# Causal mask of the first attention: added in the accumulator by VectorE instead of a TensorE product of the unit matrix with the mask

## The reference

```python
s = jnp.einsum("bhqd,bhkd->bhqk", qi, kh).astype(jnp.float32) * scale
s = s + ci[..., :, None] - c[:, :, None, :]
q_pos = i * Q_BLOCK + jnp.arange(Q_BLOCK)
s = jnp.where(k_pos[None, :] <= q_pos[:, None], s, -jnp.inf)
p = jax.nn.softmax(s, axis=-1).astype(vh.dtype)
return jnp.einsum("bhqk,bhkd->bhqd", p, vh)
```

## Time and profile before

| | |
|---|---|
| median of 3 runs | 2807.35 us |
| lowest, highest | 2804.43, 2808.54 us |
| span of the profiled execution | 2800.1 us |
| TensorE busy | 2668.2 us, 95% |
| VectorE busy | 1814.9 us, 65% |
| ScalarE busy | 1261.1 us, 45% |
| GpSimd busy | 400.7 us, 14% |
| mean granted clock of TensorE | 0.984 of full |

### The profile page before, as it was taken

The page is one execution under the profiler, slowest core; times in us unless marked ns, Lnnn a source line. Parts: engine busy times, 40 slices in busy tenths (PEclk is TensorE's granted clock), DMA queues, the critical chain, the costliest instruction groups (busy, mean ns, idle before and its releaser), DMA issues. The chain is left out here.

```text
span 2800.1 us, 35787 instructions
## 1 busy us (share of the span) xinstructions
PE 2668.2 (95%) x13585; PEld 2229.8 (80%) x13585; DVE 1814.9 (65%) x2331; ACT 1261.1 (45%) x1900; POOL 400.7 (14%) x578
## 2 busy tenths in 40 slices
PE   8999999999999999999999999989999499999995
PEld 7788888888897777778888898868878488888884
DVE  4277776632347888884343542378854798888887
ACT  4244443421244333333232422168842377777774
POOL 2011110000021222221010220012231300000102
PEclk9999999999999999999999999999999799999998
DMA  5100010111323435547441632000233699999996
GB/s 182 34 24 12 12 35 16 53 54 52 113 84 104 137 115 159 163 140 277 155 143 53 184 87 64 20 20 20 72 122 125 247 376 395 393 396 394 396 396 237
DMA packets 245593, 424.40 MB, mean 152 GB/s; under 512 B 15164, under 2 KB 161328, under 8 KB 245424
## 3 DMA queue, kind: packets, MB, share of 16 engines
q1 hardware_dynamic: 222304, 349.06, 35.3%
q0 software_dynamic: 23008, 73.03, 8.2%
q10 hardware_dynamic: 112, 0.03, 0.0%
HBM read 367.48 MB, written 45.14 MB: 147 GB/s over the span
## 5 line engine op out<-in xcount | busy, mean ns | idle before, releaser
L497 PE MATMUL ps<-r,r 128*128 128x512 f32 (+2 forms) x10448 | 2302.9, 378 | 21.5 <-ACT f L786 4.4
L497 PEld LDWEIGHTS ps<-r,r 128*128 128x128 f32 x10448 | 1870.0, 189 | 375.9 <-issue 14.7
L474 ACT ACTIVATE r<-f 128x2048 fp32r<-128x2048 f32 (+2 forms) x319 | 486.2, 1531 | 422.5 <-PE ps L497 405.0
L3541 DVE TENSOR_TENSOR r<-f,r 128x2048 fp32r<-128x2048 f32 x188 | 429.3, 2292 | 63.7 <-ACT r L474 62.6
L482 DVE TENSOR_TENSOR r<-f,r 128x1024 fp32r<-128x1024 f32 (+1 forms) x131 | 144.6, 1117 | 372.3 <-ACT r L474 371.9
L497 PE MATMUL ps<-f,f 128*128 128x64 f32 (+3 forms) x1410 | 218.4, 304 | 0.4 <-DVE f L3489 0.3
L497 PEld LDWEIGHTS ps<-f,f 128*128 128x128 f32 (+1 forms) x1410 | 179.5, 192 | 23.2 <-issue 19.6
L831 DVE SCALAR_TENSOR_TENSOR f<-f,misc,f 128x1023 f32<-128x1023 f32 (+29 forms) x120 | 146.4, 1262 | 0.0
L1764 DVE SCALAR_TENSOR_TENSOR f<-f,misc,f 128x256 f32<-128x256 f32 x224 | 128.6, 594 | 8.4 <-DMA f<-in_w_ada_dram 6.1
L1909 ACT ACTIVATE r<-f 128x512 fp32r<-128x512 f32 x140 | 87.6, 629 | 76.4 <-PE ps L497 63.2
L1115 ACT ACTIVATE f<-ps,misc 128x128 f32<-128x128 f32 (+7 forms) x64 | 47.5, 742 | 146.1 <-DVE misc L1104 146.1
(11 more groups left out here) (335 smaller groups left out, 2112.2 us busy)
## 6 DMA issues: line engine op xcount, KB each, us to landing
f<-in_w_gate_dram SPq DMA_DIRECT2D x64, 1024.0 KB, 8.6
f<-in_w_up_dram SPq DMA_DIRECT2D x64, 1024.0 KB, 10.3
f<-in_w_down_dram SPq DMA_DIRECT2D x64, 1024.0 KB, 8.4
f<-in_w_in_dram SPq DMA_DIRECT2D x56, 512.0 KB, 4.5
f<-in_w_ada_dram SPq DMA_DIRECT2D x48, 512.0 KB, 3.9
f<-hid_scratch SPq DMA_DIRECT2D x44, 512.0 KB, 5.2
f<-in_w_ffn_in_dram SPq DMA_DIRECT2D x80, 256.0 KB, 4.5
x_scratch<-f POOLq DMA_DIRECT2D x24, 512.0 KB, 5.1
```

Source lines behind the costliest of these rows:

```text
L474: self.act.activation(hi, raw, ACT.Copy).then_inc(self.sem(st.name + "_hi"), 1)
L497: return self.pe.matmul(o, left, right, start=start, stop=stop, skip_group_check=True)
L3541: self.dve.tensor_tensor(es.lo[i % 4], es.raw[i % 8], es.hi[i % 4].bitcast(F32), ALU.subtract).then_inc(self.sem("e_lo"), 1)
```

## The change

The product with the mask is gone from `pe_scores`; each score product now closes its own group, and the last one raises `at_qk`. In `dve_largest` VectorE, after its waits, adds the mask (fp32, as GpSimd made it) to the last 128 columns in the accumulator, raises a new semaphore `at_mask`, waits for it itself, and then takes the maximum. ScalarE's rounding of the mask at the start is gone, with its count of `round`.

```diff
-    (("round", 2), ("n1_sq", 8), ("pj_v", 32), ("a2_val", 32), ("hi_hi", 32)),
+    (("round", 1), ("n1_sq", 8), ("pj_v", 32), ("a2_val", 32), ("hi_hi", 32)),
...
-        self.ident_r, self.mask_r = [nc.alloc_sbuf_tensor_at(f"round{j}", [P, P], F32R, offset=base + 201 * 1024 + j * P * 4)
-                                     for j in (0, 3)]
+        self.ident_r = nc.alloc_sbuf_tensor_at("round0", [P, P], F32R, offset=base + 201 * 1024)
...
         act.activation(self.ident_r[:, 0:P], self.eye, ACT.Copy).then_inc(sem("round"), 1)
-        act.activation(self.mask_r[:, 0:P], self.mask, ACT.Copy).then_inc(sem("round"), 1)
...
-        pe.wait_ge(*sem("round", 2))
+        pe.wait_ge(*sem("round", 1))
...
             w = min(512, kw - c0)
-            diag = c0 + w == kw
             o = self.ps[:, b0 + c0 // 512, 0:w]
-            m = self.mm(o, self.QT[0:66, h, i * P:(i + 1) * P], self.KT[0:66, h, c0:c0 + w], True, not diag)
-            if diag:
-                m = self.mm(o[:, w - P:w], self.ident_r[:, 0:P], self.mask_r[:, 0:P], False, True)
+            m = self.mm(o, self.QT[0:66, h, i * P:(i + 1) * P], self.KT[0:66, h, c0:c0 + w], True, True)
         m.then_inc(sem("at_qk"), 1)
...
-        dve.tensor_reduce(self.nmax[u % 2], self.scores_of(u)[1], AX.X, ALU.max, negate=True).then_inc(
-            sem("at_max"), 1)
+        scores = self.scores_of(u)[1]
+        diagonal = scores[:, self.UNITS[u][0] * P:]
+        dve.tensor_tensor(diagonal, diagonal, self.mask, ALU.add).then_inc(sem("at_mask"), 1)
+        dve.wait_ge(*sem("at_mask", 16 * g + u + 1))
+        dve.tensor_reduce(self.nmax[u % 2], scores, AX.X, ALU.max, negate=True).then_inc(sem("at_max"), 1)
```

## The result

The changed kernel takes 2817.76 us (median of 6 runs, 2814.78 to 2820.77), the kernel before 2807.31 us on the same chip. The ratio is 1.0038 with a 95% interval of 1.0026 to 1.0049: slower by 10.5 us, 7 to 14 by the interval. The forecast was 2819.2, 11.8 us slower.

A forecast was written before the change was run, and what follows sets the result against it. A loop through VectorE's reduce, ScalarE's queue and TensorE bounds the attention. Per head pair 3.84 - 0.48 - 0.27 = 3.09 us, four make 12.4, less 0.6 gives 11.8; 2807.35 + 11.8 = 2819.2 us, range 2811.5 to 2828.

The forecast's parts named there:

- Rival (a): First attention: TensorE sets the pace, adds fall into VectorE's idle time, 3.8 us saved, 2803.5; chances 0.03 faster, 0.03 within.
- the 0.32 of the forecast: VectorE before each reduce: add 0.285 us plus 0.035 for the semaphore wait makes the maximum 0.32 us later per step.
- Rival (c): VectorE's add costs 0.425 us because it must write the accumulator as well as read it; 6.7 us more, 2826; chance 0.13.
- 12 of 16 per head pair: Attention adds on the path: u=1, 2, 4, 7 swallowed, the other 12 count, u=0 included; 12 x 0.32 = 3.84 us.
- the idle time before u=6: VectorE's gap before the reduce of u=6 swallows 0.21 us per head pair, with 0.06 in smaller gaps.
- the tail's 0.6: Last five units of head pair 3: some 0.1 us per step hides behind TensorE's previous matmul, 0.6 us less.
- as said for u=1: Add of u=1 in each head pair swallowed: VectorE next waits 0.51 us at L1182 for TensorE's values.
- 8 x 0.06 x 4: Removed mask products give back 0.06 us at eight units per head pair where the path runs through the scores.
- The rest at nothing: Mask rounding at the start gains nothing, at most 0.5 us; behind the attention everything shifts along, else up to 11.8 could vanish.
- (b): Attention: the loop binds everywhere, no add swallowed, no product back; 64 x 0.32 = 20.5 us, 2827.8; chance 0.12.
- (d): Attention: more is swallowed, only the 32 wide steps count, 6.9 or 4.5 us, 2812 to 2814; chance 0.15.
- (e): TensorE's clock: longer waits in the attention cause one drop to 1.2 GHz, costing about 4 us, 2823; chance 0.03.

The follow-up runs named there:

- the run with both: Kernel before, keeping its mask product, with the add and its wait also put ahead of the reduce; stretch 341.3 us, median 2821.6, ratio 1.0045.
- the first profile: Kernel before, unchanged, the profile on which the forecast rests; stretch from first to last reduce of the attention 329.4 us, span 2800.1.
- the second profile: Kernel before, unchanged, profiled once more for the spread between executions; stretch from first to last reduce of the attention 328.7 us.

## Why the prediction was right, step by step

**The mechanism.** TensorE is held behind the reduce by way of ScalarE's queue; the add lengthens that chain. Shown: the waits grew at the two places named, the loss is there with the product in place, and it vanishes (0.4 us the other way, within the spread) when one of the two copies is taken from behind the exponential. Rival (a), TensorE sets the pace, is out; so is its record of 465 ns. The product was worth 0.050 to 0.061 us. The 81 ns of the Trainium skill (TensorE: Matmul & The Clock Gate, section on the back-to-back issue gap), which would make 5.2 us of the 3.2 to 3.9, are not borne out here.

**The add.** It took 0.299 us and the reduce began 0.034 behind it; a step of 0.334 against the 0.32 of the forecast. Rival (c), 0.425 for a write into the accumulator, is out: writing the accumulator cost 0.015 us more than writing SBUF in L1032's group. The estimate of 0.42 per step from the Trainium skill (Perfetto Trace Analysis, section Optimizing Scalar/DVE Operations) is out with it.

**Which adds count.** This is the step of the sum that was off. The forecast had 12 of 16 per head pair, 3.84 less 0.27 of idle time. I followed the finish of the reduces unit by unit through the run with both, in head pair 2: u=0 and u=1 add 0.33 and 0.34, by u=2 and u=3 0.31 of that is gone again, and u=4, 7 and 9 to 15 add 0.31 to 0.34 each. That makes 3.31 us. The forecast's own sum, without the products and with 0.334, is 12 x 0.334 - 0.27 = 3.74. Of the 0.43 too many, 0.334 is u=0, which I had let count through the wide transposes. The other 0.09 is a misreading of the idle time before u=6: an instruction of VectorE that waits for nothing begins 0.09 before the one ahead ends, so the 0.21 of the earlier trace rows had room for 0.30. The failure at u=0 can be read from the trace. Before the change (head pair 2, the same step) TensorE waited twice in a row:

```profile
310.45 0.42 PEld L1133 LDWEIGHTS ps<-round,f 128*128 128x128 f32 x4 [0.44 <-ACT f L1142]
...
311.19 0.14 PEld L1063 LDWEIGHTS ps<-round,f 128*66 128x66 f32 x2 [0.32 <-ACT f L1013]
```

and after it

```profile
315.82 0.42 PEld L1131 LDWEIGHTS ps<-round,f 128*128 128x128 f32 x4 [0.88 <-ACT f L1140]
...
316.23 0.42 PEld L1061 LDWEIGHTS ps<-round,f 128*66 128x66 f32 x4
```

The first wait grew as forecast, and the second disappeared. The copy of v for which the second one waits follows VectorE's normalised q and k, which wait for GpSimd's power, and GpSimd's power follows L1024, which stands ahead of the add:

```profile
310.88 0.27 ACT L1013 COPY f<-ps 128x128 f32<-128x128 f32 x1 [0.48 <-DVE f L1034]
```

```profile
315.91 0.27 ACT L1011 COPY f<-ps 128x128 f32<-128x128 f32 x1
```

It starts 1.82 us behind L1024 in both traces (309.06 before, 314.09 after), although the reduce now ends 0.33 later behind L1024. So the copy did not move, and its wait swallowed what the first had gained. VectorE's lateness went at L1182, as said for u=1. The run without the adds of u=0 and u=1 agrees: no change. The sum so mended is 4 x 3.31 = 13.2, less the tail's 0.6 (in the changed kernel the last three units added 0.12, 0.10 and 0.13 in place of 0.3), 12.6; 11.9 were measured against the first profile and 12.6 against the second. The two differ in head pair 1. There the changed kernel gave only 1.93 us against the first profile, and 2.85 and 2.84 in pairs 0 and 2. Half a us of it is the wait for weights at u=12. What is left is the 0.26 us of idle time ahead of the reduce of u=14, which stands in both profiles of the kernel before and not in the changed one; the profile names nothing that it waits for, and what causes it is not settled.

**The products.** Forecast 8 x 0.06 x 4 = 1.9, measured 2.1. I had not seen that about all 64 count (3.2 to 3.9) where no add stands.

**The two together.** Adds, with the tail taken off, 13.7 forecast, 11.9 measured; products 1.9 forecast, 2.1 measured; 11.8 became 9.8 in the stretch (10.5 against the second profile) and 10.5 between the medians. The range held, and so did the sign. That the forecast comes within 1.3 us of the median is in part luck: 48 adds at 0.014 us too little make 0.7 too low, and the count of the adds was 4 x 0.43 = 1.7 us too high.

**The rest at nothing.** The stage's start moved by 0.26 us, which includes the first add. Behind the attention, up to 780 us, the same instructions start 10.0 us later throughout, so TensorE's stretch without gaps passed the delay on. One sign did not come: the time from the attention's end to the last instruction was to stay within 1 us, and it is 5.9 longer than in the first profile of the kernel before and 2.0 longer than in the second, a spread that the prediction did not know of. One reading of the profile was wrong too. The median lies 7.2 us above the span of 2800.1, but what lies outside the span is only 1.4 to 1.6 us in every run that has both numbers; by the other 5.7 or so the profiled execution ran shorter than the median. The forecast did not suffer, since it adds its 11.8 to the median.

**Rivals (b), (d), (e).** (b), all adds and no product, 20.5 us: out. (d), only the wide steps: they gave 7.9 alone and the narrow ones 0.7 alone (8.6 and 1.4 against the second profile), so (d) was nearer the truth than the chance of 0.15 said; its 6.9 us are 1.0 to 1.7 below what the wide adds alone cost, and it has nothing for the narrow ones. (e): the granted clock stayed at 1.00 through the attention in both kernels.

## What to carry to other kernels

A queue in order makes everything behind an instruction wait for what that instruction waits for: before moving work to an engine that is idle half the time, look at which engine's queue stands behind it, and first take short copies that others need out from behind a long instruction that has slack itself. Here two such exchanges were worth 11 us in the attention (8 to 11 us in the time of the whole kernel) and made the moved work nearly free. In a sum along a loop, check at each wait whether its other inputs move as well; two waits in a row of which one has a fixed cause swallow a delay.

## What the runs showed of the hardware

- A 128x128 add of VectorE with both an operand and the result in the accumulator took 0.299 us, one from the accumulator to SBUF 0.284. A second instruction that needs the result begins 0.034 us after the end; one that doesn't begins 0.21 after the start of the first, before it ends.
- A fp32r product of 128 columns between fp32 ones cost 0.050 to 0.061 us of TensorE's time, while its record says 0.465 on average.
- From the last reduce of the attention to the end, the 14 profiles differ by up to 11.5 us (2329.2 to 2340.7) though nothing was changed there, more than the effect studied. Inside the attention one late weight transfer (a wait of 0.75 us on ScalarE) made a stretch of 329 us 0.5 longer.
